# The four recurrence tiles of the prompt in one unrolled stage, each staged between the levels of the tile ahead

## The reference

```python
def step(S, inp):
    r_t, w_t, k_t, v_t, kk_t, a_t = inp
    sa = jnp.einsum('bhij,bhj->bhi', S, -kk_t)
    S = (S * w_t[:, :, None, :] + sa[..., None] * (kk_t * a_t)[:, :, None, :]
         + v_t[..., None] * k_t[:, :, None, :])
    return S, jnp.einsum('bhij,bhj->bhi', S, r_t)
S_T, o = lax.scan(step, wkv0.astype(f32), xs)
```

## Time and profile before

| | |
|---|---|
| median of 3 runs | 5326.66 us |
| the profiled execution's own time | 5332.04 us |
| its span, first to last instruction | 5330.2 us |
| TensorE busy | 4778.4 us (90%) |
| mean granted TensorE clock | 0.943 |
| from the first staging to the last output copy of the prompt's recurrence, first layer | 391.38 to 510.84 us |

### The profile page before, as it was taken

The page is one execution under the profiler, slowest core; times in us unless marked ns, Lnnn a source line. Parts: engine busy times, 40 slices in busy tenths (PEclk is TensorE's granted clock), DMA queues, the critical chain, the costliest instruction groups (busy, mean ns, idle before and its releaser), DMA issues. The chain is left out here.

```text
span 5330.2 us, 99808 instructions
## 1 busy us (share of the span) xinstructions
PE 4778.4 (90%) x39364; PEld 4586.7 (86%) x39364; DVE 3141.6 (59%) x6341; ACT 1670.6 (31%) x2570; POOL 363.3 (7%) x194
## 2 busy tenths in 40 slices
PE   7768596999999999999987676969899999999998
PEld 7647496899999999999985465969899999999998
DVE  3564478875555555557735644888755555555576
ACT  2322222882222222222123222228722222222222
POOL 0200054000000000000002000540000000000000
PEclk9878798999999999999998787989999999999999
DMA  3330121664333333325323301216743333333253
GB/s 96 109 143 1 61 97 47 179 199 179 115 120 133 116 115 116 131 111 177 119 86 125 120 2 70 90 45 192 210 164 130 115 115 117 135 117 115 105 196 120
DMA packets 390832, 631.24 MB, mean 118 GB/s; under 512 B 29184, under 2 KB 327680, under 8 KB 348800
## 3 DMA queue, kind: packets, MB, share of 16 engines
q1 hardware_dynamic: 388640, 620.74, 33.1%
q10 hardware_dynamic: 2016, 8.26, 0.4%
HBM read 526.52 MB, written 152.36 MB: 127 GB/s over the span
## 5 line engine op out<-in xcount | busy, mean ns | idle before, releaser
L228 PE MATMUL ex_op<-ex_ah,ex_vl 128*128 128x288 f32 x3584 | 1066.6, 298 | 7.4 <-DVE ex_acc L2305 6.4
L230 PE MATMUL ex_op<-ex_ah,ex_vh 128*128 128x288 f32 x3584 | 1057.7, 295 | 0.0
L229 PE MATMUL ex_op<-ex_al,ex_vh 128*128 128x288 f32 x3584 | 1056.1, 295 | 0.0
L2305 DVE TENSOR_TENSOR ex_acc<-ex_acc,ex_op 128x576 f32<-128x576 f32 x896 | 672.6, 754 | 549.0 <-PE ex_op L230 535.0
L228 PE MATMUL ex_hp<-x_hi,ex_ul 128*128 128x288 f32 x3072 | 906.2, 295 | 18.4 <-PEq L122 15.8
L230 PE MATMUL ex_hp<-x_hi,ex_uh 128*128 128x288 f32 x3072 | 907.1, 295 | 0.0
L229 PE MATMUL ex_hp<-x_lo,ex_uh 128*128 128x288 f32 x3072 | 906.2, 295 | 0.0
L228 PEld LDWEIGHTS ex_op<-ex_ah,ex_vl 128*128 128x128 f32 x3584 | 674.2, 188 | 14.9 <-DVE ex_acc L2305 14.9
L230 PEld LDWEIGHTS ex_op<-ex_ah,ex_vh 128*128 128x128 f32 x3584 | 673.8, 188 | 0.0
L229 PEld LDWEIGHTS ex_op<-ex_al,ex_vh 128*128 128x128 f32 x3584 | 673.1, 188 | 0.0
L2254 ACT ACTIVATE ex_vh<-ex_v 128x2048 fp32r<-128x2048 f32 x128 | 245.6, 1918 | 1138.1 <-PE ex_op L230 858.7
(11 more groups left out here) (414 smaller groups left out, 8843.1 us busy)
## 6 DMA issues: line engine op xcount, KB each, us to landing
ex_u<-in_peer_uT SPq DMA_DIRECT2D x128, 1024.0 KB, 7.7
ex_v<-in_peer_v SPq DMA_DIRECT2D x128, 1024.0 KB, 6.8
gate_matrix<-g_stage SPq DMA_DIRECT2D x18, 4096.0 KB, 15.9
ex_g<-gate_matrix SPq DMA_DIRECT2D x128, 576.0 KB, 4.9
dec_k<-in_cache_kT SPq DMA_DIRECT2D x16, 1536.0 KB, 10.4
dec_v<-in_cache_v SPq DMA_DIRECT2D x16, 1536.0 KB, 8.0
out_s_k<-in_cache_k_kept SPq DMA_DIRECT2D x128, 190.5 KB, 6.2
out_s_v<-in_cache_v_kept SPq DMA_DIRECT2D x128, 190.5 KB, 6.2
```

The source lines that it names most:

```text
L228: nc.tensor.matmul(out, w_lo, x_hi, start=first, stop=False)
L229: nc.tensor.matmul(out, w_hi, x_lo, start=False, stop=False)
L230: return nc.tensor.matmul(out, w_hi, x_hi, start=False, stop=last)
L2305: nc.vector.tensor_tensor(a, a, o[:, :, 0:HALF], ALU.add).then_inc(s.added, 1)
```

## The change

The device loop over tiles is gone. `rwkv_prompt` is one stage for the four tiles, unrolled; so the block, its clearing block and the loop's branch are passed once instead of four times. The staged tensors `kr`, `ki`, `bi`, `ke`, `be`, `vs` and `dc` have two buffers, used by turns. Tile 0 is staged ahead of everything, as before. Tile i + 1 is staged on VectorE in five parts, one behind the two adds of each level of tile i; the last part has two instructions (`ke` and `be`). ScalarE copies `vs` of tile i + 1 behind tile i's last power. TensorE's list of tile i + 1 follows tile i's directly, with two waits that are new: for tile i's last output copy ahead of the third Gram product (banks 2/3), and for the last state addition ahead of the transposes (banks 6/7). Semaphore counts run on over the tiles. The number of arithmetic instructions that are executed, and their sizes, stay the same; slices are constants where they were computed from the loop's register.

The diff, cut where lines only gain an indentation or a running count:

```diff
-def rwkv_prompt_tile(nc, m, r, tile):
-    t = bass.ds(tile * P, P)
+def rwkv_prompt(nc, m, r):
+    TILES = TP_ // P
...
-        kr = sb("rp_kr", [P, PAIRS, 2, P])
-        ki, bi = sb("rp_ki", [P, PAIRS, P]), sb("rp_bi", [P, PAIRS, P])
-        ke, be, vs = sb("rp_ke", [P, PAIRS, P]), sb("rp_be", [P, PAIRS, P]), sb("rp_vs", [P, PAIRS, P])
-        dc = sb("rp_dc", [P, PAIRS, NC])
+        kr2 = sb("rp_kr", [P, 2, PAIRS, 2, P])
+        ki2, bi2, ke2, be2, vs2 = (sb("rp_" + n, [P, 2, PAIRS, P]) for n in ("ki", "bi", "ke", "be", "vs"))
+        dc2 = sb("rp_dc", [P, 2, PAIRS, NC])
...
             @block.vector
             def _(dve):
                 st = Steps(dve, s.dve_step)
-                nc.vector.tensor_tensor(kr[:, :, 0, :], r.kk[:, :, t], r.prev[:, :, t], ALU.mult)
...
+                def stage_part(i, part):
+                    t, x = slice(i * P, (i + 1) * P), i % 2
+                    kr = kr2[:, x]
+                    if part == 0:
+                        if i >= 2:
+                            dve.wait_ge(s.o_made, (i - 1) * NC)
+                        nc.vector.tensor_tensor(kr[:, :, 0, :], r.kk[:, :, t], r.prev[:, :, t], ALU.mult)
+                    elif part == 1:
+                        nc.vector.tensor_tensor(kr[:, :, 1, :], r.r[:, :, t], r.cum[:, :, t], ALU.mult)
+                    elif part == 2:
+                        nc.vector.tensor_tensor(bi2[:, x], r.b[:, :, t], r.inv[:, :, t], ALU.mult).then_inc(s.staged, 1)
+                    elif part == 3:
+                        nc.vector.tensor_tensor(ki2[:, x], r.k[:, :, t], r.inv[:, :, t], ALU.mult).then_inc(s.staged, 1)
+                    elif part == 4:
+                        nc.vector.tensor_tensor(ke2[:, x], r.k[:, :, t], r.end[:, :, t], ALU.mult)
+                        nc.vector.scalar_tensor_tensor(out=be2[:, x], in0=r.b[:, :, t], scalar=-1.0, in1=r.end[:, :, t],
+                                                       op0=ALU.mult, op1=ALU.mult).then_inc(s.staged, 1)
+
+                for part in range(5):
+                    stage_part(0, part)
+                for i in range(TILES):
...
+                    for k in range(LEVELS):
+                        for a in range(2):
+                            dve.wait_ge(s.folded, 2 * (i * LEVELS + k) + a + 1)
...
+                        if i + 1 < TILES:
+                            stage_part(i + 1, k)
...
             @block.scalar
...
+                def values(i):
+                    if i >= 2:
+                        act.wait_ge(s.turned, 4 * (i - 1))
+                    copy(vs2[:, i % 2], r.v[:, :, i * P:(i + 1) * P]).then_inc(s.v_staged, 1)
+
+                values(0)
+                for i in range(TILES):
...
+                    for k in range(1, LEVELS):
+                        for a in range(2):
+                            power(k, a)
+                    if i + 1 < TILES:
+                        values(i + 1)
...
             @block.tensor
...
+                for i in range(TILES):
+                    x = i % 2
+                    kr, ki, bi, ke, be, vs = (y[:, x] for y in (kr2, ki2, bi2, ke2, be2, vs2))
...
+                    pe.wait_ge(s.staged, 3 * i + 1)
+                    gram(0, lambda q, c, w: bi[q, c, w], both, 2 * CH)
+                    gram(4, lambda q, c, w: kr[q, c, 0, w], lambda q, c, w: bi[q, c, w], CH)
+                    pe.wait_ge(s.staged, 3 * i + 2)
+                    if i:
+                        pe.wait_ge(s.o_in, i * NC)
+                    gram(2, lambda q, c, w: ki[q, c, w], both, 2 * CH)
+                    pe.wait_ge(s.staged, 3 * i + 3)
+                    pe.wait_ge(s.v_staged, i + 1)
+                    if i:
+                        pe.wait_ge(s.st_in, i * NC)
...
@@ rwkv
-        with nc.Fori(0, TP_ // P) as i:
-            rwkv_prompt_tile(nc, m, r, i)
+        rwkv_prompt(nc, m, r)
```

More of the change, by code:

```diff
@@ L1229, in _ @@
[L1229 to L1250, removed]
-                    for a in range(2):
[L1252 to L1255, removed]
@@ L1278, in copy @@
                     return nc.scalar.activation(out, src, ACT.Copy)
[L1280 to L1304, removed]
+                def values(i):
[4 more added lines that the diff above has]
+                for i in range(TILES):
+                    for src in range(4):
+                        act.wait_ge(s.turned, 4 * i + src + 1)
+                        copy(tok[:, src, :], ps[:, 6 + src % 2, 0:H3]).then_inc(s.turned_in, 1)
+                    def power(k, a):
+                        act.wait_ge(s.powers, 2 * (i * LEVELS + k) + a + 1)
+                        b = slice(0, 2) if k < LEVELS - 1 else slice(1, 2)
+                        copy(n_m[:, a, :, b, :], ps[:, a, 0:PAIRS * 2 * CH].rearrange("p (c b w) -> p c b w", c=PAIRS, b=2)
+                             [:, :, b, :]).then_inc(s.powers_in, 1)
+                    act.wait_ge(s.tt_made, i + 1)
+                    power(0, 0)
+                    power(0, 1)
+                    act.wait_ge(s.bv_made, i + 1)
+                    copy(bv[:].rearrange("p a c i -> p (a c i)"), ps[:, 6, 0:H3]).then_inc(s.bv_in, 1)
+                    for k in range(1, LEVELS):
[3 more added lines that the diff above has]
+                        values(i + 1)
+                    act.wait_ge(s.uv_made, i + 1)
+                    copy(uv[:].rearrange("p a c i -> p (a c i)"), ps[:, 4, 0:H3]).then_inc(s.uv_in, 1)
+                    for n in range(NC):
+                        q = rows[n]
+                        act.wait_ge(s.o_made, i * NC + n + 1)
+                        copy(output(i)[q], blocks(2, HD)[q]).then_inc(s.o_in, 1)
@@ L1306, in _ @@
             @block.tensor
             def _(pe):
[L1308 to L1330, removed]
@@ L1378, in _ @@
-                fold(LEVELS - 1, 1)
-                pe.wait_ge(s.added, 2 * LEVELS)
-                for c in range(PAIRS):
-                    for a in range(2):
-                        h = 2 * c + a
-                        for n in range(NC):
-                            q = rows[n]
-                            ins = nc.tensor.matmul(ps[half[a], 5 + 2 * n, c * CH:(c + 1) * CH],
-                                                   tok[q, 0, h * HD:(h + 1) * HD], tt[q, a, c, :], start=True, stop=True)
@@ new lines, in fold @@
+                        ins.then_inc(s.folded, 1)
+                    for k in range(LEVELS):
+                        square(k, 0)
+                        if k:
+                            fold(k - 1, 1)
+                        square(k, 1)
+                        if k == 0:
+                            pe.wait_ge(s.turned_in, 4 * i + 4)
+                            pe.wait_ge(s.bq_made, i + 1)
+                            for a in range(2):
+                                for c in range(PAIRS):
+                                    h = 2 * c + a
+                                    for q in rows:
+                                        ins = nc.tensor.matmul(ps[q, 6, (a * PAIRS + c) * HD:(a * PAIRS + c + 1) * HD],
+                                                               bq[q, a, c, 0, :], tok[q, 3, h * HD:(h + 1) * HD],
+                                                               start=True, stop=True)
+                            ins.then_inc(s.bv_made, 1)
+                        fold(k, 0)
@@ L1430, in _ @@
-                    ins.then_inc(s.o_made, 1)
+                            for n in range(NC):
+                                q = rows[n]
+                                ins = nc.tensor.matmul(ps[half[a], 5 + 2 * n, c * CH:(c + 1) * CH],
+                                                       tok[q, 0, h * HD:(h + 1) * HD], tt[q, a, c, :], start=True, stop=True)
+                    ins.then_inc(s.wt_made, 1)
+                    pe.wait_ge(s.bv_in, i + 1)
+                    for a in range(2):
+                        for c in range(PAIRS):
+                            for q in rows:
+                                ins = nc.tensor.matmul(ps[q, 4, (a * PAIRS + c) * HD:(a * PAIRS + c + 1) * HD],
+                                                       tt[q, a, c, :], bv[q, a, c, :], start=True, stop=True)
```

221 lines of the change are left out of this document (119 added, 102 removed).

## The result

| | before | after |
|---|---|---|
| median | 5328.09 us (5 runs) | 5288.01 us (5 runs); 5286.10 us for the four that count (5280.55 to 5292.51) |
| ratio, four against five | | 0.992, 95% interval 0.9904 to 0.9935 |
| profiled execution, time | 5332.04 us | 5284.18 us |
| span | 5330.2 us | 5282.4 us |
| first staging to last output copy, layer 1 | 119.46 us | 386.71 to 485.68, 98.97 us |

One run of the changed kernel was disturbed (6098 us, granted clock 0.732) and does not count. A second measurement of the same kernel, a control for a later experiment, gave 5290.79 us against 5326.01 and 0.9936 (0.9922 to 0.9949). So the change takes 35 to 42 us by the medians; it was forecast at 38.0.

The account below looks back on a forecast made before the run. No engine full, no transfer hidden: cuts in the chain of work shorten the run. Edges 14.2, Gram products 4.5, transposes 0.9, less 0.6 for `wt`: 19.0 us a layer, 38.0 in two, from 5326.66 to 5288.7 us; range 5282 to 5301.

Parts of the forecast that it names:

- The edges: Between tiles: without meetings and bare staging, the next tile's first Gram product starts 4.74 us sooner.
- The clock: Gram products of tiles 1 to 3: at full instead of half clock, 1.90 us for 3.41, gaining 1.5 us each.
- The output copy: Third Gram product at a tile edge: its new wait for the last output copy costs 0, margin 0.0 to 0.3 us.
- `wt`: End of a tile's levels: the last staging part delays `wt` and so TensorE's state part by 0.2 us, bounds 0 to 0.94.
- The instruction loads: Unrolled prompt stage: some 5 code loads for each tile, 30 more in all, hidden beside the work, cost 0.
- The sum: One layer's prompt stage: tile 0 25.71 us, tiles 1 and 2 24.21 each, tile 3 24.77; gain 19.0 us.
- (b): Rival: edges go, but the clock falls in each tile's state part or transposes; 5299.5 us, chance 0.15.
- (c): Rival: VectorE's staging in the levels delays adds that TensorE waits for, 16.9 us in all; 5305.6 us, chance 0.05.
- (d): Rival: only the meetings go, staging or output copy still stands at the tile edge, 14.6 us gained; 5312, chance 0.02.
- (e): Rival: slower, TensorE stands at each of 30 new instruction loads for 2.4 us, 72 us; 5360.7 us, chance 0.03.
- (f): Rival: constant slices or the missing loop entry give a few tenths at more places than the edges; 5281, chance 0.02.

Follow-up runs that it names:

- the idle: Changed kernel with TensorE standing still at each edge between tiles, waiting for ten short ScalarE copies; 5324.8 us.
- filled edge: Changed kernel with a wait at each tile edge for ten ScalarE copies, TensorE meanwhile making 20 matmuls that nobody reads; 5316.0 us.
- late staging: Changed kernel with all staging of a tile at that tile's own head on VectorE, none inside the levels of the tile ahead; 5292.8 us, ratio 0.9936.
- kernel with both steps: Changed kernel with staging earlier, the next tile's second Gram product in the state part and the third behind the first six transposes; 5284.41 us, ratio 0.9924.
- unrolled kernel: Kernel before with its loop over tiles unrolled and nothing else, four stages with their meetings kept; 5321.46 us, ratio 0.9986.
- kernel filled with 40: Changed kernel with a wait at each tile edge for ten ScalarE copies, TensorE making 40 matmuls that nobody reads; 5343.9 us.
- the early Gram product: Changed kernel with staging earlier and the next tile's second Gram product made in this tile's state part; 5284.7 us, ratio 0.992.
- early parts: Changed kernel with four staging parts ahead of the tile's first add, `ke` and `be` behind levels 0 and 1; 5288.03 us, ratio 0.9927.

## Why the prediction was right

- **The edges, 4.74 us.** Right: no meeting and no staging is left between tiles. The joined stage without interleaving already gives all but 0.7 us an edge, and all but 2.3 where it loses the clock. Unrolling with the meetings kept leaves 4.0 to 4.5 us of wait.
- **The clock, 1.5 us a tile.** Right, and shown by the idle and the filled edge: 1.65 us with the transposes. The Gram products took 415.35 - 413.37 = 1.98 us where I had 1.90, while 1.82 is their pace with nothing ahead of them (late staging, filled edge). The 0.16 us between is not a wait. The first product starts among the last four matmuls of tile 0 and shares TensorE with them: its last matmul ends at 414.41, 1.04 us behind its start, where late staging has 0.89. The kernel with both steps has 1.05 too (412.73 + 0.87 against 412.55), and there no third product stands behind the first.
- **The output copy, 0 with a margin of 0.0 to 0.3 us.** Right, with nothing to spare. The third product comes up 1.05 us behind the first here and 1.05 with late staging, where the copy had ended 1.2 us before. That there is no margin shows as soon as the second product leaves the edge.
- **`wt`, 0.2 us.** Mechanism right, size 0.15.
- **The instruction loads, 0.** Right: 20 loads stand in the stage, as forecast, in the unrolled kernel and in the changed one. The argument for it was weaker than it looked: tile 3 of the kernel before was 0.39 us longer than tile 0, loads or none, because its clock rose later (4.5 us behind its first Gram product, in tile 0 3.6). The unrolled stages settle it.
- **The sum.** 19.0 us a layer was forecast from first staging to last copy, 20.5 measured. Tile 0's pitch was put at 25.71 and is 413.37 - 388.26 = 25.11: 0.17 of the 0.60 is a clock that rose sooner in this execution (Gram products in 3.24 us instead of 3.41), 0.05 the transposes, 0.06 `wt`. The rest is in the state part, `wt`'s first user to the next tile: 413.37 - 406.52 = 6.85 against 418.44 - 411.27 = 7.17. There the second tile's matmuls start before the last of the first have gone out (0.23 us, where I let them queue behind; 0.16 of it comes back in the longer Gram products), and the output copy of the tile's first chunk comes 0.1 us sooner, which the unrolled stages show too, with constant slices and nothing joined. With 0.37 in each of the two next tiles (23.84 against 24.21) and 0.15 in the last this is the 1.5. The terms were off by some tenths at most, mostly to the same side; the stages give 41.2 us for 38.0. That the first median, 5288.01, comes within 0.7 us of the forecast is luck: the four undisturbed runs give 5286.10, the control 5290.79.
- **The rivals.** (b) is out by the windows for this kernel, but its mechanism is real and near: the clock fell behind a pause of 0.64 us with late staging, and in the state part of one tile of the kernel filled with 40. (c) and (d): no add that TensorE waits for was late, and no idle time is left at the edge. (e) is out by the unrolled stages. (f) had something in it: unrolling alone, constant slices and no branch, shortens the stages by 2.1 us over both layers.

## What to carry to other kernels

When a loop's body is a stage of its own, price the whole edge: the meeting, the first work that runs bare behind it, and the slow clock that the pause leaves for TensorE's next few microseconds, which stands in no list of waits and shows only in the matmuls' durations. Joining the passes takes all three. Then put the staging inside the pass ahead as well: left at the edge it was bare for only 0.65 us, but at one edge in three that short pause was enough to lose the clock again. Then look at the next wait on the joined list before you move more work forward: the early Gram product brought a third of its length until the product that waits for the output copy was moved too.

## What the hardware showed beside this

- The length of a pause alone does not say whether the clock falls. Behind 0.64 or 0.65 us of TensorE it was 1.00 at four edges and 0.50 at two, behind 0.38 us 1.00, behind 2.48 us 0.50, and once it fell with no pause over 0.46 us. What decides between equal pauses was not tried.
- A 128x128 matmul of f32 by f32 is two entries in the trace, 0.12 us each at full clock (40 in 4.73 us), where a transpose is one. I had counted one, and sized a filling at half its length by it.
- The unchanged sample stage took from 29.97 to 31.84 us in the kernels here, alike in both layers of one kernel. It starts at half clock each time, and it is short where the clock rises soon: 4.3, 4.0 and 3.9 us behind the stage's start it took 30.06 (unrolled), 30.41 (filled with 20) and 30.37 us (second product early), while 6.4 us (before), 6.6 (control) and 6.9 (early parts) go with 31.58, 31.60 and 31.76. What moves the rise stays open. Over two layers this is up to 3.4 us, nearly as much as the two last steps gained, so such steps are read from their own stage.
